# Gathering 32 columns per token block first, and the whole gather behind the first expert pair's gate and up products

## The chip, the core and the metric

The kernel runs on one core of a Trainium2 chip. The core has a matrix engine (PE, with its weight loads shown apart as PEld), a vector engine (DVE), a scalar engine (ACT), GpSimd (POOL), an engine that here only issues transfers (SP), and sixteen DMA engines that bring data from HBM. The engines run their own instruction lists and wait for each other by semaphores. The metric is device time in microseconds for one call; lower is better.

## The reference

The program is two transformer blocks on 256 tokens of 1024 channels, in float32. The first block has two kinds of attention and then a mixture of 32 experts; the second a recurrent mixer and a dense feed-forward network. The change touches the start of the expert layer:

```python
g_sel = argmax(t @ w_group + b_group)                # one of 4 groups for each token
top_v, top_i = top_k(logits of the 8 experts of that group, 2)
w_top = softmax(top_v) * p_group
hg = einsum('nd,edf->nef', t, w_gate)                # each expert: 1024 -> 256
hu = einsum('nd,edf->nef', t, w_up)
a  = silu(hg) * hu * comb[:, :, None]                # comb is 0 but for a token's two experts
y  = einsum('nef,efd->nd', a, w_down)                # 256 -> 1024
```

So only two of 32 experts count for a token, 512 (token, expert) pairs in all.

## The kernel before

The kernel computes only the pairs that are chosen. Each token block (BLK = 2 blocks of 128 tokens) has 256 chosen pairs; a pair gets a column, sorted by expert within its block. `cols` holds each token's two columns. `pick[:, b, :]`, 128 tokens by 256 columns of zeros and ones, is made on DVE by comparing a row of column numbers with `cols` (L2398 to L2405). The gather is a product on PE: for each of KT = 8 tiles of 128 channels and each block, `tok` (normed tokens, 128 tokens by 128 channels) times `pick` gives the block's columns of that tile in a PSUM bank. One bank (512 columns) holds both blocks of one tile, so the gather fills all eight banks with 32 matmuls (L1194 to L1207). ACT moves the even tiles to `xsT` and adds a shift (L1871), DVE the odd ones (L2460).

The experts are then worked off in 16 teams of two (TEAMS). A team's input is a window of 64 columns (WIN): 32 columns (SUB) of each block from the place where its two experts start. `copy_window` (L2446) copies it from `xsT` to `xw`. For the first team it is done in two parts, tiles 0 to 5 and 6 to 7 (FIRST_TILES = 6), so that its products can begin early. If a team has more than 32 columns in a block, a flag selects another, slower branch; here it is the quick one.

One team on the quick branch is: gate and up products in bank 0 (L1210, 32 matmuls with 64-wide stationary tiles and 512 columns), Silu on ACT (L1884), the product of gate and up with the row mask on DVE (L2848), two transposes on PE (`turn_act`, L1270), a copy on ACT (L1889), the down products in bank 2 (L1284, 16 matmuls), and copies of their result by ACT and DVE. While PE is at it, DVE copies the next team's window and makes the matrix that later adds the rows back to their tokens (`put_rows_joined`, L2428). The adding back (L1299) fills gaps of PE.

DVE has a list of its own between the gather and the first Silu: row numbers, masks and weights of all experts (L2475 to L2519). At its end it lets ACT start the first Silu.

The weights of six experts (HOMES) are in SBUF at a time: four in a ring, one in `hs`, one (expert 5, then 11 and so on) partly in `tok`, which is also the gather's input. SP issues the transfers in a written order, each with the wait that frees its place. Around the change: expert 2 (L624), two quarters of expert 5 into `tok`, each behind a part of the gather (L626 to L629), then for experts 6 and 7 the first halves of gate and up, as soon as the first half of the first team's products is done (L638), the second halves when all of them are done (L643), the down weights after the first team's down products (L650), then expert 8 and so on, each after a team's products. Two semaphores carry this: `gate_up_used` and `chunk_used`.

Of the kernel before, what the change touches and what calls it, by code (L numbers as in the profile page):

```python
# [112 lines left out]
FIRST_TILES = 6  # L113
# [42 lines left out]
def build(nc, x, c, w_ada, b_ada, g_mix, w_in, b_forget, g_out_a, g_out_b, w_out, g_ffn, w_group,  # L156
# [3 lines left out]
    with ExitStack() as ctx:  # L160
# [341 lines left out]
        def _(sp):  # L502
# [123 lines left out]
            sp.wait_ge(gather_done, 1)  # L626
            load_quarter(5, 0, 0)
            sp.wait_ge(gather_done, 1 + KT)
            load_quarter(5, 1, 0)  # L629
# [140 lines left out]
        def _(pe):  # L770
# [423 lines left out]
            def gather():  # L1194

                pe.wait_ge(htr_taken_a, 4)
                for b in range(BLK):
                    pe.wait_ge(pick_ready, b + 1)
                    for j in range(KT):
                        if b == 0 and j == 6:  # L1200
                            pe.wait_ge(row_taken, 8)
                        last = pe.matmul(ps[:, j, b * L:(b + 1) * L], lhsT=tok[:, b, j * P:(j + 1) * P], rhs=pick[:, b, :],
                                         start=b == 0, stop=b == BLK - 1, skip_group_check=True)
                        if b == BLK - 1:
                            last.then_inc(gather_done, 1)
                    if b == 0:
                        last.then_inc(gather_done, 1)  # L1207
# [430 lines left out]
            with pe.Else():  # L1638
                gather()
# [25 lines left out]
        def _(act):  # L1665
# [205 lines left out]
            def take_gathered():  # L1871

                for j in range(0, KT, 2):
                    act.wait_ge(gather_done, j + 2)
                    act.activation(xsT[:, j, 0:PAIRS], ps[:, j, :], ACT.Identity, bias=shift_q[:, j:j + 1]
                                   ).then_inc(gather_taken_a, 1)

            def team_act(n, u, fast):
# [1027 lines left out]
```

## Time and profile before

| | us |
|---|---|
| time, median of 3 runs | 766.99 (766.43 to 768.08) |
| profiled execution, its time | 765.26 |
| profiled execution, its span | 762.7 |
| PE busy | 730.6 (96%) |
| DVE busy | 354.0 (46%) |
| ACT busy | 188.0 (25%) |
| POOL busy | 58.8 (8%) |
| mean granted clock of PE | 0.999 of 2.4 GHz |

The span reaches from the first to the last instruction; the time has 2.56 us more around it. The expert layer's stage reaches from some 188 us (routing) to 420 us of the span. A row of a timeline gives start and length in us, engine, line, what is written and read, how often, and in brackets how long the engine was idle before it and what ended the wait.

### The profile page before, as it was taken

What the parts mean: (1) busy time and instruction counts of PE and PEld (TensorE: products, weight loads), DVE (VectorE), ACT (ScalarE), POOL (GpSimd) and SP (SyncE); (2) the same over time, 40 slices, a digit from 0 to 9 for tenths busy, and PEclk for the clock granted to TensorE, in tenths of its full rate; (3) what the DMA queues carried; (4) which work ended last, traced back from release to release, by engine and by line L of the source; (5) the groups of instructions that cost most, each with busy time, mean ns of one, the idle gap of its engine ahead of it and who ended that gap; (6) DMA issues with size and microseconds to landing.
All of it is one profiled execution on the core that took longest, in us unless ns stands there. A gap on an engine that the chain in (4) does not pass through costs nothing.

```text
span 762.7 us, 9761 instructions
## 1 busy us (share of the span) xinstructions
PE 730.6 (96%) x3883; PEld 485.9 (64%) x3883; DVE 354.0 (46%) x798; ACT 188.0 (25%) x412; POOL 58.8 (8%) x69
## 2 busy tenths in 40 slices
PE   6999999998889999999989999999999999999996
PEld 4677778786524434343334886788888888885442
DVE  2125666785721212121121876364276656567445
ACT  5014323533511111111011338131321111111002
POOL 3033660040000000000001000000000000000000
PEclk9999999999999999999999999999999999999999
DMA  9998956956999999999999963123454645443401
GB/s 339 339 339 249 396 192 222 354 205 261 351 377 415 416 414 416 418 413 415 419 409 368 371 227 111 46 66 111 151 181 135 197 146 185 157 175 111 165 28 58
DMA packets 78250, 197.27 MB, mean 259 GB/s; under 512 B 3343, under 2 KB 38520, under 8 KB 72312
## 3 DMA queue, kind: packets, MB, share of 16 engines
q1 hardware_dynamic: 77248, 195.37, 68.6%
q10 hardware_dynamic: 664, 0.80, 0.4%
q0 software_dynamic: 288, 0.41, 0.3%
q8 instruction: 33, 0.54, 0.3%
q14 instruction: 17, 0.14, 0.1%
HBM read 195.33 MB, written 1.05 MB: 257 GB/s over the span
## 4 chain that ended last, share of the span: by engine, by line
PE 75%; SPq 10%; DMA 7%; DVE 5%; ACT 1%; issue 1%; POOL 1%; DVEq 0%; ACTq 0%
PE ps L1502 18%; PE ps L1218 9%; PE ps L777 9%; PE ps L1563 9%; PE ps L1294 5%; PE ps L903 4%; PE ps L1127 4%; SPq L572 4%; PE ps L914 2%; DMA arena<-in_w_up 2%; DMA ring<-in_w_ada 2%; SPq L578 2%; PE ps L1089 2%; PE ps L1099 2%; DMA ring<-in_w_in 2%; PE ps L1303 2%
## 5 line engine op out<-in xcount | busy, mean ns | idle before, releaser
L1218 PE MATMUL ps<-ring,arena 128*64 128x512 f32 x352 | 77.6, 593 | 3.1 <-DMA ring<-in_w_up 2.5
L903 PE MATMUL ps<-hs,ring 128*128 128x256 f32 (+1 forms) x288 | 66.2, 384 | 1.0 <-DMA ring<-in_w_in 1.0
L903 PEld LDWEIGHTS ps<-hs,ring 128*128 128x128 f32 (+1 forms) x288 | 52.7, 187 | 12.7 <-issue 3.8
L1218 PEld LDWEIGHTS ps<-ring,arena 128*64 128x64 f32 x352 | 26.3, 137 | 52.5 <-issue 52.5
L2848 DVE SCALAR_TENSOR_TENSOR arena<-arena,own_rows,ps 128x256 f32<-128x256 f32 x16 | 7.7, 480 | 106.8 <-ACT arena L1884 106.8
L777 PE MATMUL ps<-hs,ring 128*128 128x256 f32 x240 | 53.3, 381 | 0.3 <-PE ps L777 0.3
L777 PEld LDWEIGHTS ps<-hs,ring 128*128 128x128 f32 x240 | 45.2, 190 | 7.1 <-issue 0.9
L1502 PE MATMUL ps<-ring,hs 128*128 128x256 f32 x176 | 41.7, 380 | 0.9 <-DVE xT L2727 0.9
L1502 PE MATMUL ps<-ring,mixT 128*128 128x256 f32 x176 | 41.7, 380 | 0.0
L1502 PE MATMUL ps<-arena,mixT 128*128 128x256 f32 x176 | 41.6, 379 | 0.0
L1294 PE MATMUL ps<-ring,arena 128*64 128x512 f32 x176 | 40.2, 598 | 1.0 <-issue 0.5
L1218 PE MATMUL ps<-hs,arena 128*64 128x512 f32 x80 | 35.2, 592 | 2.2 <-DMA arena<-in_w_up 2.2
L1502 PEld LDWEIGHTS ps<-ring,hs 128*128 128x128 f32 x176 | 33.3, 190 | 6.1 <-issue 1.7
L1502 PEld LDWEIGHTS ps<-arena,mixT 128*128 128x128 f32 x176 | 33.4, 190 | 4.5
L1502 PEld LDWEIGHTS ps<-ring,mixT 128*128 128x128 f32 x176 | 32.6, 190 | 4.0
L1884 ACT ACTIVATE arena<-ps 128x256 f32<-128x256 f32 x16 | 6.1, 384 | 108.4 <-PE ps L1218 100.7
L1127 PE MATMUL ps<-mixT,ring 128*128 128x256 f32 x128 | 28.0, 380 | 0.1
L2690 DVE TENSOR_TENSOR arena<-ring 128x1024 f32<-128x1024 f32 x16 | 19.5, 1220 | 15.7 <-PE ps L1563 15.7
L1294 PEld LDWEIGHTS ps<-ring,arena 128*64 128x64 f32 x176 | 11.9, 136 | 23.1 <-issue 22.4
L1127 PEld LDWEIGHTS ps<-mixT,ring 128*128 128x128 f32 x128 | 24.2, 190 | 3.7 <-issue 0.5
L1218 PEld LDWEIGHTS ps<-hs,arena 128*64 128x64 f32 x80 | 10.9, 137 | 24.4 <-issue 24.4
L2856 DVE COPY arena<-ps 64x512 f32<-64x512 f32 x12 | 8.2, 683 | 36.6 <-PE ps L1294 36.6
(483 smaller groups left out, 1215.5 us busy)
## 6 DMA issues: line engine op xcount, KB each, us to landing
ring<-in_w_down SPq DMA_DIRECT2D x23, 1024.0 KB, 18.1
ring<-in_w_gate_up SPq DMA_DIRECT2D x22, 1024.0 KB, 7.2
ring<-in_w_gate SPq DMA_DIRECT2D x18, 1024.0 KB, 17.1
ring<-in_w_up SPq DMA_DIRECT2D x18, 1024.0 KB, 17.9
ring<-in_w_ada SPq DMA_DIRECT2D x5, 3072.0 KB, 12.9
ring<-in_w_down SPq DMA_DIRECT2D x5, 2048.0 KB, 8.1
ring<-in_w_in SPq DMA_DIRECT2D x9, 1024.0 KB, 17.1
ring<-in_w_ada SPq DMA_DIRECT2D x16, 512.0 KB, 9.3
```

The lines of the kernel that those rows point to most:

```text
L572: sp.dma_start(dst, src[:, e, :]).then_inc(arrived[e % HOMES], 16)
L578: sp.dma_start(dst, src[:, e, D:2 * D] if far else src[:, e, 0:D]).then_inc(arrived[SLOTS + 1], 16)
L777: last = pe.matmul(o, lhsT=w_of(k), rhs=rhs_of(k), start=k == 0, stop=k == k_n - 1)
L903: last = pe.matmul(o[0:n, 0:L], lhsT=w[:, k, lo:lo + n], rhs=h[:, k, :], start=k == 0, stop=k == KT - 1)
L914: last = pe.matmul(o[:, i * n:(i + 1) * n], lhsT=hT[:, k, b * P:(b + 1) * P], rhs=w[:, k, lo:lo + n], start=k == 0, stop=k == KT - 1 and f ...
L1089: last = pe.matmul(ps[:, m // 2, (m % 2) * L:(m % 2 + 1) * L], lhsT=w[:, k, (m % 4) * P:(m % 4 + 1) * P], rhs=mixT[:, k, :], start=m % 2 = ...
L1127: last = pe.matmul(o, lhsT=w[:, k, (m % 4) * P:(m % 4 + 1) * P], rhs=mixT[:, k, :], start=last_of is None and m % 2 == 0 and k % 4 == 0, s ...
L1218: last = pe.matmul(ps[WIN * h:WIN * (h + 1), 0, :].rearrange("p (g n) -> p g n", g=2), lhsT=xw[:, u, k, :], rhs=expert_gate_up(2 * n + h, ...
L1294: last = pe.matmul(ps[WIN * half:WIN * (half + 1), 2, :], lhsT=act_turned[:, u, at:at + WIN], rhs=expert_down(2 * n + h)[:, k, lo:lo + 512 ...
L1502: last = pe.matmul(o, lhsT=tokens(k), rhs=columns(k), start=start and k == 0, stop=k == 3, skip_group_check=True)
L1563: last = pe.matmul(ps[:, DOWN_BANK[name], :], lhsT=lhsT, rhs=rhs, start=n == 0, stop=n == FT // 2 - 1, skip_group_check=True)
L2690: ve.tensor_tensor(sums[0], lo_2, lo_1, ALU.subtract).then_inc(weight_sums, 1)
```

## The change

The first team's window always starts at column 0 of each block, so its columns are known without the window's start. The change makes these 32 columns of each block's pick first and gathers them alone, into halves of two banks (`gather_first`); DVE adds the shift and writes them as the first team's window. The rest of the picks follows on DVE. The first team's gate and up products come next on PE. The whole gather is done in the order of the tiles: two tiles behind those products, six behind the turn of the activations, in banks that are free beside banks 0, 1 and 2 (GATHER_BANKS). Its evictions go between the first team's steps on ACT and DVE, and DVE's second window is copied after them. The down products of the first team now also wait for the tile in bank 2 to be taken. On SP the two quarters of expert 5 that lie in `tok` go behind the second halves of experts 6 and 7 and wait for the whole gather. The slower branch keeps the whole gather; it does the first gather besides.

```diff
-FIRST_TILES = 6
+FIRST_TILES = 4
+GATHER_BANKS = (2, 3, 4, 5, 6, 7, 3, 4)
@@ -623,10 +624,6 @@
-            sp.wait_ge(gather_done, 1)
-            load_quarter(5, 0, 0)
-            sp.wait_ge(gather_done, 1 + KT)
-            load_quarter(5, 1, 0)
@@ -641,6 +638,9 @@
                 if team == HOMES // 2:
                     load_early_halves(1)
+                    sp.wait_ge(gather_done, 2 + KT)
+                    load_quarter(5, 0, 0)
+                    load_quarter(5, 1, 0)
@@ -1191,20 +1191,36 @@
+            def gather_first():
+                pe.wait_ge(htr_taken_a, 4)
+                for half, bank in enumerate((3, 1)):
+                    for b in range(BLK):
+                        if half == 0:
+                            pe.wait_ge(pick_ready, b + 1)
+                        for i in range(FIRST_TILES):
+                            j = half * FIRST_TILES + i
+                            last = pe.matmul(ps[:, bank, i * WIN + b * SUB:i * WIN + (b + 1) * SUB],
+                                             lhsT=tok[:, b, j * P:(j + 1) * P], rhs=pick[:, b, 0:SUB],
+                                             start=b == 0 and i == 0, stop=b == BLK - 1 and i == FIRST_TILES - 1,
+                                             skip_group_check=True)
+                    last.then_inc(gather_done, 1)
+            def gather(tiles):
+                for j in tiles:
+                    if j == 0:
+                        pe.wait_ge(pick_ready, 2 * BLK)
+                        pe.wait_ge(first_windows, 2)
+                    if GATHER_BANKS[j] == 6:
+                        pe.wait_ge(row_taken, 8)
+                    if j >= 6:
+                        before = GATHER_BANKS.index(GATHER_BANKS[j])
+                        pe.wait_ge(gather_taken_v if before % 2 else gather_taken_a, before // 2 + 1)
+                    for b in range(BLK):
+                        last = pe.matmul(ps[:, GATHER_BANKS[j], b * L:(b + 1) * L], lhsT=tok[:, b, j * P:(j + 1) * P],
+                                         rhs=pick[:, b, :], start=b == 0, stop=b == BLK - 1, skip_group_check=True)
+                    last.then_inc(gather_done, 1)
@@ -1614,13 +1630,16 @@
+            gather_first()
             with pe.If(too_many < 1):
-                gather()
                 weights_there(0)
                 gate_up(0, 0, first=True).then_inc(gu_done, 1)
+                gather((0, 1))
                 pe.wait_ge(act_ready, 2)
                 turn_act(0)
+                gather(range(2, KT))
                 pe.wait_ge(turn_taken, 1)
+                pe.wait_ge(gather_taken_a, 1)
                 down_joined(0)
@@ -1868,25 +1887,29 @@
                 act.activation(act_g, ps[:, 0, 0:FE], ACT.Silu).then_inc(silu_done, 1)
+                if first:
+                    take_gathered((0,))
                 act.wait_ge(turn_done, n + 1)
...
                 act.activation(act_turned[:, u, :], ps[:, 1, 0:FE], ACT.Copy).then_inc(turn_taken, 1)
+                if first:
+                    take_gathered((2, 4, 6))
@@ -2396,13 +2418,25 @@
+                ve.tensor_scalar(tmp_cols[:, b * SUB:(b + 1) * SUB], col_no[:, b * L:b * L + SUB], cols[:, 1, b:b + 1], None,
+                                 ALU.is_equal).then_inc(dve_step, 1)
+            for b in range(BLK):
+                own()
+                ve.scalar_tensor_tensor(pick[:, b, 0:SUB], col_no[:, b * L:b * L + SUB], cols[:, 0, b:b + 1],
+                                        tmp_cols[:, b * SUB:(b + 1) * SUB], ALU.is_equal, ALU.add).then_inc(pick_ready, 1)
...
+            for half, bank in enumerate((3, 1)):
+                tiles = slice(half * FIRST_TILES, (half + 1) * FIRST_TILES)
+                ve.wait_ge(gather_done, half + 1)
+                ve.tensor_tensor(xw[:, 0, tiles, :], ps[:, bank, 0:FIRST_TILES * WIN].rearrange("p (k n) -> p k n", n=WIN),
+                                 shift_q[:, tiles].unsqueeze(2).broadcast_to([P, FIRST_TILES, WIN]), ALU.add
+                                 ).then_inc(first_windows, 1)
@@ -2460,18 +2494,14 @@
             starts = load(0, 2 * BLK)
-            take_gathered((1, 3, 5))
-            copy_window(0, starts[0:BLK], slice(0, FIRST_TILES)).then_inc(first_windows, 1)
-            take_gathered((7,))
-            copy_window(0, starts[0:BLK], slice(FIRST_TILES, KT)).then_inc(first_windows, 1)
@@ -2847,7 +2877,11 @@
+                    if n == 0:
+                        put_rows_joined(1)
+                        take_gathered(range(1, KT, 2))
+                        copy_window(1, starts[BLK:2 * BLK]).then_inc(windows_copied, 1)
```

## Rows read from the trace of the kernel before

**Rows 1.** The page's busy times: us, share of the span, instructions.
```profile
PE 730.6 (96%) x3883; PEld 485.9 (64%) x3883; DVE 354.0 (46%) x798; ACT 188.0 (25%) x412; POOL 58.8 (8%) x69
```
**Rows 2.** The chain that ended last, 184 to 420 us: start us, us, what.
```profile
211.80 0.39 ACT arena L1884
...
213.67 3.65 PE ps L1294 x16
217.32 6.89 PE ps L1218 x32
...
371.72 18.31 DMA arena<-in_w_up
```
**Rows 3.** The waits, 185 to 420 us: who, for whom, us, times, longest.
```profile
PE ps L1218 <- DMA ring<-in_w_up: 2.5, 2, 1.8
PE ps L1218 <- DMA arena<-in_w_up: 2.2, 1, 2.2
```
**Rows 4.** Stretches: us, busy times of PE to POOL, PEclk, DMA share, GB/s.
```profile
185.00:190.00 5.00, 2.99 (x27) 2.07 (x24) 3.13 (x11) 1.29 (x4) 0.74 (x1) 1.00 0.86 308
198.00:207.00 9.00, 8.36 (x39) 5.84 (x39) 5.20 (x17) 4.11 (x6) 0.00 (x0) 1.00 1.01 397
207.00:209.00 2.00, 2.00 (x12) 0.86 (x10) 1.73 (x9) 0.00 (x0) 0.00 (x0) 1.00 0.47 193
209.00:213.00 4.00, 2.77 (x14) 0.89 (x10) 2.62 (x11) 0.38 (x1) 0.00 (x0) 1.00 0.88 241
213.00:219.00 6.00, 5.53 (x28) 1.91 (x28) 1.58 (x6) 0.98 (x2) 0.00 (x0) 1.00 1.01 372
...
300.00:390.00 90.00, 85.28 (x396) 34.30 (x392) 17.11 (x56) 11.73 (x29) 0.00 (x0) 1.00 1.02 416
390.00:404.00 14.00, 13.84 (x64) 6.13 (x66) 2.22 (x8) 1.31 (x3) 0.52 (x1) 1.00 1.03 409
```
**Rows 5.** The timeline around the gather and the first team, 191 to 216 us.
```profile
195.31 0.29 DVE L2395 TENSOR_REDUCE arena<-arena 128x4 f32<-128x128 f32 x1
...
196.65 7.14 PE L1202 MATMUL ps<-arena,tok 128*128 128x256 f32 x32 [0.91 <-DVE arena L2404]
...
197.34 0.76 DVE L2409 TENSOR_SCALAR wins_i<-arena 1x32 int32<-1x32 f32 x8
...
204.44 7.09 PE L1218 MATMUL ps<-ring,arena 128*64 128x512 f32 x32 [0.64 <-DVE arena L2449]
...
205.35 0.29 DVE L2477 TENSOR_TENSOR rank<-arena 128x32 f32<-128x32 f32 x2
...
208.12 0.33 SPq L635 DMA_DIRECT2D ring<-in_w_gate  x1
...
212.76 0.44 PE L1273 MATMUL ps<-ident,arena 128*128 128x128 f32 x2 [1.23 <-DVE arena L2848]
```
**Rows 6.** The timeline: rows elsewhere that are nearest to the new operations.
```profile
188.85 1.92 PE L1171 MATMUL ps<-ident,hs 128*128 128x128 f32 x16
...
204.21 0.75 DVE L2464 TENSOR_SCALAR arena<-ps,small 128x512 f32<-128x512 f32 x1
...
208.49 0.86 DVE L2505 SCALAR_TENSOR_TENSOR w_all<-arena,w_all 128x32 f32<-128x32 f32 x4
...
226.72 0.50 DVE L2449 COPY arena<-arena 128x256 f32 x2 [1.49 <-issue]
...
435.76 1.08 DVE L2556 TENSOR_TENSOR arena<-ps,rstd 128x256 f32<-128x256 f32 x3
```
**Rows 7.** Timeline at 224 us; DMA issues (count, KB, landing) of 217, 224, 378.
```profile
224.27 0.34 SPq L572 DMA_DIRECT2D ring<-in_w_gate  x1
...
ring<-in_w_down SPq DMA_DIRECT2D x2, 1024.0 KB, 9.5
...
ring<-in_w_gate SPq DMA_DIRECT2D x1, 1024.0 KB, 6.6
...
ring<-in_w_gate SPq DMA_DIRECT2D x4, 512.0 KB, 15.6
```

More of the change, by code:

```diff
@@ L1192, in _ @@
             quarters(6, ones[:, 0:Q], w[:, PE_K, :], last=True).then_inc(ada_rows_done, 1)
-            def gather():
+            def gather_first():
                 pe.wait_ge(htr_taken_a, 4)
[L1197 to L1207, printed above, removed]
+                for half, bank in enumerate((3, 1)):
[9 more added lines that the diff above has]
+                    last.then_inc(gather_done, 1)
@@ L1638, in _ @@
             with pe.Else():
-                gather()
+                gather(range(KT))
                 clear_banks()
@@ L1869, in _, with take_gathered, team_act @@
             too_many = act.value_load(flag_i[0:1, 0:1], min_val=0, max_val=1)
[L1871 to L1875, printed above, removed]
+            def take_gathered(tiles):
+                for j in tiles:
+                    act.wait_ge(gather_done, j + 3)
+                    act.activation(xsT[:, j, 0:PAIRS], ps[:, GATHER_BANKS[j], :], ACT.Identity, bias=shift_q[:, j:j + 1]
                                    ).then_inc(gather_taken_a, 1)
-            def team_act(n, u, fast):
+            def team_act(n, u, fast, first=False):
                 act.wait_ge(gu_done, n + 1)
@@ L2048, in _ @@
             with act.If(too_many < 1):
-                take_gathered()
                 for n in range(TEAMS):
-                    team_act(n, n % 2, True)
+                    team_act(n, n % 2, True, n == 0)
                 second_block()
             with act.Else():
-                take_gathered()
+                take_gathered(range(0, KT, 2))
                 with act.Fori(0, TEAMS * WINDOWS) as i:
@@ L2398, in _ @@
             for b in range(BLK):
-                if b:
-                    ve.wait_ge(pick_ready, b)
-                half, found = col_no[:, b * L:(b + 1) * L], tmp_cols
+                ve.tensor_scalar(tmp_cols[:, b * SUB:(b + 1) * SUB], col_no[:, b * L:b * L + SUB], cols[:, 1, b:b + 1], None,
[4 more added lines that the diff above has]
+                                        tmp_cols[:, b * SUB:(b + 1) * SUB], ALU.is_equal, ALU.add).then_inc(pick_ready, 1)
+            for b in range(BLK):
+                ve.wait_ge(pick_ready, BLK + b)
+                half, found = col_no[:, b * L + SUB:(b + 1) * L], tmp_cols[:, SUB:L]
                 ve.tensor_scalar(found, half, cols[:, 1, b:b + 1], None, ALU.is_equal).then_inc(dve_step, 1)
                 own()
-                ve.scalar_tensor_tensor(pick[:, b, :], half, cols[:, 0, b:b + 1], found, ALU.is_equal, ALU.add
+                ve.scalar_tensor_tensor(pick[:, b, SUB:L], half, cols[:, 0, b:b + 1], found, ALU.is_equal, ALU.add
                                         ).then_inc(pick_ready, 1)
+            for half, bank in enumerate((3, 1)):
[4 more added lines that the diff above has]
+                                 ).then_inc(first_windows, 1)
             starts_4d = starts_f.rearrange("p (b q h) -> p b q h", b=BLK, h=2)
@@ L2462, in take_gathered @@
                 for j in tiles:
-                    ve.wait_ge(gather_done, j + 2)
-                    ve.tensor_scalar(xsT[:, j, 0:PAIRS], ps[:, j, :], shift_q[:, j:j + 1], None, ALU.add
+                    ve.wait_ge(gather_done, j + 3)
+                    ve.tensor_scalar(xsT[:, j, 0:PAIRS], ps[:, GATHER_BANKS[j], :], shift_q[:, j:j + 1], None, ALU.add
                                      ).then_inc(gather_taken_v, 1)
@@ L2859, in _ @@
             with ve.Else():
+                take_gathered(range(1, KT, 2))
                 ve.memset(put[:, 0], 0.0).then_inc(dve_step, 1)
```

2 lines of the change are left out of this document (1 added, 1 removed).

## Prediction

> **What bounds the kernel now.** I read the page's busy shares first: PE is busy for 96% of the span and every other engine for less than half of it [rows 1]. That looks like a kernel whose every microsecond of PE counts, so I next read the chain that ended last over the expert stage, 184 to 420 us [rows 2]. It runs over PE with steps of ACT between them at first (the Silu at 211.80, the down products at 213.67, the next team's gate and up products at 217.32), but further on it leaves PE: it goes through SP's issues and a transfer, "DMA arena<-in_w_up", of 18.31 us from 371.72. The waits say the same in small: between 185 and 420 us gate and up products waited for weights three times, 2.5 us on ring tiles (two waits) and 2.2 us on an arena tile [rows 3]. So by 390 us PE has caught up with the weight stream, and the end follows the stream and not PE. The table of stretches shows why: from 300 to 390 us the sixteen DMA engines move 416 GB/s with a share of 1.02 [rows 4]. A team's weights are six transfers of 1024 KB, 6.29 MB, or 15.1 us at 416; a team's products take some 12.9 us on PE (two starts of gate and up, 204.44 [rows 5] and 217.32 [rows 2], are 12.88 apart). PE lives on a head start that is used up at 390.
>
> The question is therefore what the change does to the stream, and the place to look is the only stretch behind the gather that is not full: 207 to 209 with 193 GB/s and a share of 0.47, 209 to 213 with 241 and 0.88, 213 to 219 with 372 and 1.01 [rows 4]. SP sits before the first early halves until the first half of the first team's gate and up products is done; they go out at 208.12 [rows 5], when the queue has run dry.
>
> **The change part by part. PE and DVE first, as they set SP's issues.**
> The columns of the tokens are known when the reduction of 195.31 ends, 195.60 [rows 5]. Before, two full pick rows follow until 197.34 (1.74 us), and the gather starts in their midst at 196.65.
>
> *Short picks (added):* four operations of 32 columns; the nearest row has four of 128x32 in 0.86 [rows 6]. First pick after three of them, 196.25, second 196.46. PE starts some 0.15 after the first: 196.4.
>
> *First gather (added):* 16 matmuls with 128-wide stationary tiles and 32 moving columns. No row has them. Bounds: the 16 transposes with the same stationary width in 1.92, and the full gather, 32 in 7.14, that is 0.223 each [rows 5, 6], so 1.9 to 3.6 us. I take 1.9, since 32 columns are nearer to the transposes' 128 than to 256. First half done at 197.4, second at 198.3.
>
> *Rest of the picks (moved behind):* 224 of 256 columns, so at most the 1.74 of before, from 196.46 to 198.2. DVE, not PE, is late here. Then two adds from PSUM of 128x256, three of which took 1.08 [rows 6]: 198.6 and 198.95. They stand where the gather's evictions and the two window copies stood.
>
> *Gate and up products of the first team* start at 198.7 instead of 204.44 [rows 5], 5.7 earlier, and end 7.1 later at 205.8. PE's branch now stands between first gather and products; the 0.4 us in which PE waits for DVE cover it.
>
> *DVE's list to the first Silu (not changed, but now exposed):* the window starts, eight short operations in 0.76 [rows 5], the register loads, bounded by the 1.49 us idle "issue" ahead of a window copy in the team loop [rows 6], and then everything from 205.35 [rows 5] to the Silu at 211.80 [rows 2], 6.45. From 198.95: 198.95 + 0.76 + 1.49 + 6.45 = 207.65, say 207.7. The products end at 205.8, so PE's two gather tiles (4 matmuls, 0.9) fit into the wait for nothing, and of the 5.7 us only 211.80 - 207.7 = 4.1 are left. This is the new wait that takes the gather's place.
>
> *Rest of the gather (moved):* the first two tiles cost nothing, by that wait. The other 12 matmuls, 12 x 0.223 = 2.7, stand between turning the activations and the down products. Before, the turn started 0.96 after the Silu (212.76 [rows 5]) and down 1.87 after it (213.67). Now 207.7 + 0.96 + 0.2 + 2.7 = 211.55: a gain of 2.1 against 213.67. ACT's copy of the turned activations is beside it.
>
> *Evictions (moved):* on DVE after its product (Silu + 0.9) and the put rows (0.9): four of 0.75 [rows 6], the last not before the gather's end, so 212.5, then the second window, 213.1; wanted by PE at 211.55 + 3.65 = 215.2. ACT's four lie beside. Cost nothing, with a cover of 2 us; beyond it they would hold the second team.
>
> *SP:* both quarters of expert 5 (team 2) leave the place ahead of the early halves and go behind them, past the wait for the whole gather (211.6). Behind that wait stand only the loads of team 3's down weights, which wait for the first down products (215.2) anyway. The first early halves go out 3.7 after the products' start as before (208.12 - 204.44 [rows 5]): 202.4; the second at 205.9. Team 2's products come at 227, the quarters land before 220.
>
> **The sum.** PE's gain at the second team is 2.1 us, and with it the issue of expert 8's weights, 224.27 before [rows 7], moves to 222.1. For the stream: bytes moved from 198 to 209 are 9 x 397 + 2 x 193 = 3960 KB [rows 4]; without the 1050 of the quarters the queue runs dry at 205.1, but the early halves are there from 202.4 and the second from 205.9. The dry stretch disappears. It is worth 2 x (1 - 193/416) + 4 x (1 - 241/416) = 1.07 + 1.68 = 2.75 us; 213 to 219 holds another 6 x (1 - 372/416) = 0.63 with full shares, which I leave where it is. Does the stream then run dry later, at expert 8? Before, its first transfer, issued at 224.27, landed 6.6 later at 230.9, and the last down weights before it at about 228.3 (issued to 218.9, 9.5 in the mean) [rows 7]; one transfer of 1024 KB takes 2.5, so its bytes began when those of the earlier ones ended, about 226.4 to 227 if a landing trails its bytes by 1 to 2 us. An issue moves bytes about 1 us later (208.12, after which 207 to 209 stayed at 193): it was early by 1 to 2 us. With 2.1 of PE's gain on top, the stream may gain up to 3.1 before it waits for SP. So the stream gains 2.75, and PE's waits at its end [rows 3] shrink or grow to fit. After 390 the second half of the kernel follows shifted, as its first weights stand in the same queue.
>
> The profiled execution took 765.26: 762.7 of span and 2.6 around it. Forecast for it: 762.5. It lies 1.7 below the median of the runs, 766.99; on that footing the forecast is 766.99 - 2.75 = 764.2.
>
> Rule against the change: the moved transfers are 512 KB, and 241 GB/s is what the stretch of such pieces shows [rows 4]. The Trainium skill ("DMA: Bandwidth & Descriptors", section Bandwidth) advises batching to 1 MiB or more for at least 75% of peak. By that the slow 209 to 213 would be the price of the small pieces and stay, and only the 1.07 of 207 to 209 would be won. The trace speaks against it: the last teams' eight halves of 512 KB, issued from 378 on behind others and landed 15.6 us later in the median [rows 7], move in a full stream, 409 GB/s from 390 to 404 [rows 4]. It is the empty queue, I think, not the size.
>
> **Rivals.**
> *A. The stream keeps its shape:* the slow stretch belongs to the pieces themselves and comes back a few us earlier. For it: shares of 0.88 and 1.01 at 241 and 372 GB/s are busy engines. Against: 409 in 390 to 404. Gain at most 1.07: 765.9, or nothing at all.
> *B. The whole lead reaches the end:* the 5.7 us at the first products carry through: 761.3. Against it are DVE's list to 207.7 and three waits for weights [rows 3].
> *C. The products start earlier, DVE's list does not shrink:* first gather at 3.6 us and slow register loads put the Silu at 209.1 or later; PE gains 0.7, and the stream, bound by expert 8's issue, 1.7 to 2.7: 765.3 at most. It is the low end of the forecast's own range.
> *D. Slower: TensorE's clock.* PE now waits for the picks' adds (0.4 us) and some 2 us ahead of the turn. If after this the clock falls to the lower level (1.2 GHz), the 12 matmuls and the down products take twice their 2.7 + 3.65, PE loses 6.35 - 2.1 = 4.2, and from the 1 to 2 us by which expert 8's issue was early it is the stream that loses, 2.7 at the middle: 769.7. Against: from 185 to 190 PE was busy for 2.99 of 5 us and the granted clock stayed at 1.00, the full 2.4 GHz; so in all rows shown [rows 4]. The Trainium skill ("TensorE: Matmul & The Clock Gate", section Why this matters for your kernels) warns of idle gaps between bursts; no gap of this case's stretch made it happen.
>
> **How the numbers follow.** Forecast with C 0.65 (gain 1.7 to 3.4), A 0.23, B 0.05, D 0.07. A measurement of this kernel can tell about 0.2%, 1.5 us. Faster by more: nearly all of the first and B, 0.67. Within: A and a rest, 0.25. Slower: D and a part of the unknown, 0.08. Range: below, a gain of 3.4 (all of 207 to 219) and 0.8 for the spread of the runs, 762.8; above, A with no more than 0.5 won, 766.5.
>
> **What would show it.** In the changed profile: first products at about 198.7 and the Silu about 207.7, released by DVE and not by PE; twelve gather matmuls just before the first down products at about 211.5; second team's products at 215.2; no second between 204 and 215 with less than 300 GB/s; the last wait for weights at about 387 instead of 390. The prediction is wrong if the slow second stretch is still there, if expert 8's weights go out later than 224, or if the granted clock leaves 1.00.

## The result: slower, by 0.4%

The changed kernel takes 768.99 us (median of 10 runs, 767.41 to 771.53), the one before 766.17 beside it (10 runs, 764.74 to 768.08): ratio 1.0042, 95% interval 1.0028 to 1.0056. The forecast was 764.2. The profiled execution took 767.41, with a span of 764.6; before 765.26 and 762.7. It is the fastest of its ten, so the tables below show 1.9 of the 2.8 us between the medians. The page's busy line, to be held against [rows 1]:

```profile
PE 736.3 (96%) x3915; PEld 489.7 (64%) x3915; DVE 353.5 (46%) x800; ACT 187.9 (25%) x412; POOL 59.0 (8%) x69
```

PE has 32 records more than before, 3915 against 3883, and 5.7 us more of busy time.

The view to compare next is PE's timeline around the gather (start, length, engine, line, operation, tiles, count; in brackets the idle time ahead and what ended it). L1203 is the first gather, L1234 gate and up, L1221 the rest of the gather, L1289 the turn, L1310 the down products:

```profile
196.22 3.73 PE L1203 MATMUL ps<-arena,tok 128*128 128x32 f32 x32 [0.58 <-DVE arena L2425]
199.88 8.78 PE L1234 MATMUL ps<-ring,arena 128*64 128x512 f32 x32
208.60 1.99 PE L1221 MATMUL ps<-arena,tok 128*128 128x256 f32 x8
210.43 0.38 PE L1289 MATMUL ps<-ident,arena 128*128 128x128 f32 x2
210.65 5.35 PE L1221 MATMUL ps<-arena,tok 128*128 128x256 f32 x24
215.92 3.65 PE L1310 MATMUL ps<-ring,arena 128*64 128x512 f32 x16
219.41 7.04 PE L1234 MATMUL ps<-ring,arena 128*64 128x512 f32 x32
```

The first products did move forward, from 204.44 to 199.88 [rows 5]. But the first down products moved back, from 213.67 [rows 2] to 215.92, and the second team, 217.15 in the same view of the kernel before, to 219.41 ([rows 2] has 217.32 from the chain, which counts a piece from the end of the one ahead of it):

```profile
217.15 7.04 PE L1218 MATMUL ps<-ring,arena 128*64 128x512 f32 x32
```

The rows also show why: the source has 16 products in the first gather and 12 in the rest of it, and the trace has 32 and 24 records. In every group of products here one product is two matmul records: gate and up are 16 in the source and 32 here, the down products 8 and 16. Only the transposes of the turn have one record each, 2 and 2. The "32 matmuls" and "16 matmuls" in the section on the kernel before are therefore records, and the full gather's 32 are 16 products.

DVE, ACT and SP's queue in the same stretch:

```profile
198.20 0.42 DVE L2437 TENSOR_TENSOR arena<-ps,small 128x256 f32<-128x256 f32 x1 [0.24 <-PE ps L1203]
199.99 0.42 DVE L2437 TENSOR_TENSOR arena<-ps,small 128x256 f32<-128x256 f32 x1 [1.36 <-PE ps L1203]
202.92 0.29 DVE L2507 TENSOR_TENSOR rank<-arena 128x32 f32<-128x32 f32 x2 [1.83 <-issue]
209.37 0.38 ACT L1903 ACTIVATE arena<-ps 128x256 f32<-128x256 f32 x1 [10.10 <-DVEq L2548]
205.27 0.33 SPq L632 DMA_DIRECT2D ring<-in_w_gate  x1
208.75 0.33 SPq L632 DMA_DIRECT2D ring<-in_w_gate  x1
216.02 0.33 SPq L579 DMA_DIRECT2D tok<-in_w_gate  x1
219.62 0.89 SPq L600 DMA_DIRECT2D ring<-in_w_down  x2
226.53 0.34 SPq L573 DMA_DIRECT2D ring<-in_w_gate  x1
```

DVE waits 1.36 us for the second half of the first gather; from 202.92 its list takes the forecast 6.45 us, and the Silu is let go by DVE's list ("DVEq"), at 209.37. On SP the early halves leave at 205.27 and 208.75, the quarters at 216.02, team 3's down weights at 219.62, and expert 8's weights at 226.53, 2.26 later than before [rows 7]. What that does to the weight stream stands in the table of stretches (length; busy time of each engine; PE's granted clock; DMA share; GB/s):

```profile
198.00:207.00 9.00, 9.00 (x44) 4.16 (x45) 5.16 (x28) 1.26 (x2) 0.00 (x0) 0.81 0.81 330
207.00:209.00 2.00, 2.00 (x10) 0.67 (x7) 1.46 (x6) 0.00 (x0) 0.00 (x0) 1.00 0.92 252
209.00:213.00 4.00, 4.00 (x21) 3.48 (x20) 2.35 (x7) 2.14 (x4) 0.00 (x0) 1.00 0.96 341
213.00:219.00 6.00, 6.00 (x30) 3.36 (x30) 2.33 (x5) 1.37 (x2) 0.00 (x0) 1.00 1.02 376
219.00:229.00 10.00, 8.98 (x46) 3.18 (x44) 1.56 (x4) 1.91 (x5) 0.00 (x0) 1.00 0.92 342
300.00:390.00 90.00, 87.44 (x406) 35.04 (x402) 16.43 (x55) 11.14 (x28) 0.00 (x0) 1.00 1.02 416
```

Against a full 416 GB/s these stretches are short by 9 x (1 - 330/416) = 1.86, 0.79, 0.72, 0.58 and 1.78 us, 5.7 together. Before, 198 to 219 were short by 0.41, 1.07, 1.68 and 0.63 [rows 4], 3.8, and 219 to 229 ran at 416. The difference is 1.9 us, as large as that of the spans. It comes out at the last wait for weights, of team 14:

```profile
PE ps L1234 <- DMA ring<-in_w_up: 2.3, 2, 1.8
PE ps L1234 <- DMA arena<-in_w_up: 2.1, 1, 2.1
```

The waits look as before (2.5 and 2.2 [rows 3]), which is the point: PE still waits, only later. Team 14's products start at 392.20; before at 390.16 (the first row is the kernel before, the second the changed one):

```profile
390.16 0.61 PE L1218 MATMUL ps<-hs,arena 128*64 128x512 f32 x1 [2.16 <-DMA arena<-in_w_up]
392.20 0.61 PE L1234 MATMUL ps<-hs,arena 128*64 128x512 f32 x1 [2.12 <-DMA arena<-in_w_up]
```

Up to there PE is not the bound; it only decides when SP may issue.

### The profile page after: what moved, and what is told of

Read it like the earlier page. It is cut to its first block, busy times and chain, and to the rows that moved or that the text cites. A ratio compares the mean times of both kernels' runs of the same rounds, so it can differ in the third digit from the quotient of the medians.

```text
span 764.6 us, 9824 instructions
## 1 busy us (share of the span) xinstructions
PE 736.3 (96%) x3915; PEld 489.7 (64%) x3915; DVE 353.5 (46%) x800; ACT 187.9 (25%) x412; POOL 59.0 (8%) x69
## 4 chain that ended last, share of the span: by engine, by line
PE 76%; SPq 10%; DMA 7%; DVE 4%; ACT 1%; POOL 1%; issue 1%; ACTq 0%; DVEq 0%
PE ps L1518 17%; PE ps L1234 10%; PE ps L777 9%; PE ps L1579 9%; PE ps L1310 5%; PE ps L903 4%; PE ps L1127 4%; SPq L573 4%; PE ps L914 2%; DMA arena<-in_w_up 2%; DMA ring<-in_w_ada 2%; SPq L579 2%; PE ps L1089 2%; PE ps L1099 2%; DMA ring<-in_w_in 2%; PE ps L1319 2%
## 5 line engine op out<-in xcount | busy, mean ns | idle before, releaser
L1234 PE MATMUL ps<-ring,arena 128*64 128x512 f32 x352 | 79.2, 603 | 2.3 <-DMA ring<-in_w_up 2.3
L903 PEld LDWEIGHTS ps<-hs,ring 128*128 128x128 f32 (+1 forms) x288 | 52.7, 187 | 12.9 <-issue 3.8
L1234 PEld LDWEIGHTS ps<-ring,arena 128*64 128x64 f32 x352 | 26.3, 139 | 53.1 <-issue 53.0
L1310 PE MATMUL ps<-ring,arena 128*64 128x512 f32 x176 | 40.2, 598 | 0.5 <-issue 0.5
L1234 PE MATMUL ps<-hs,arena 128*64 128x512 f32 x80 | 35.2, 592 | 2.1 <-DMA arena<-in_w_up 2.1
L1234 PEld LDWEIGHTS ps<-hs,arena 128*64 128x64 f32 x80 | 10.9, 137 | 24.4 <-issue 24.4
L1310 PEld LDWEIGHTS ps<-ring,arena 128*64 128x64 f32 x176 | 11.9, 136 | 22.7 <-issue 22.7
```

The lines of the kernel that those rows point to most:

```text
L903: last = pe.matmul(o[0:n, 0:L], lhsT=w[:, k, lo:lo + n], rhs=h[:, k, :], start=k == 0, stop=k == KT - 1)
L1234: last = pe.matmul(ps[WIN * h:WIN * (h + 1), 0, :].rearrange("p (g n) -> p g n", g=2), lhsT=xw[:, u, k, :], rhs=expert_gate_up(2 * n + h, ...
L1310: last = pe.matmul(ps[WIN * half:WIN * (half + 1), 2, :], lhsT=act_turned[:, u, at:at + WIN], rhs=expert_down(2 * n + h)[:, k, lo:lo + 512 ...
```

## The experiments

The experiments were timed in four groups, each beside the kernel before, whose medians were 767.54, 767.16, 767.22 and 767.02 us; a ratio is always to the kernel before of the same group. Two things had to be explained: which of PE's steps made SP late, and what the granted clock did, which fell to 0.51 between 200 and 202 with PE busy for all of it:

```profile
198.00:200.00 2.00, 2.00 (x20) 1.96 (x21) 0.43 (x2) 1.26 (x2) 0.00 (x0) 1.00 1.05 434
200.00:202.00 2.00, 2.00 (x6) 0.57 (x8) 1.09 (x9) 0.00 (x0) 0.00 (x0) 0.51 0.96 401
202.00:204.00 2.00, 2.00 (x8) 0.63 (x6) 0.98 (x6) 0.00 (x0) 0.00 (x0) 0.63 1.00 412
```

That is why the first team's products took 8.78 us and not 7.09.

**1. The first gather with 128 columns (FC) instead of 32.**

```diff
-                                             lhsT=tok[:, b, j * P:(j + 1) * P], rhs=pick[:, b, 0:SUB],
+                                             lhsT=tok[:, b, j * P:(j + 1) * P], rhs=pick[:, b, 0:FC],
```

> The changed kernel with a first gather that moves 128 columns of each block's pick instead of 32 (the same 32 weight loads, so the same 3.7 us on PE; only the first 32 columns of each 128 are used). Theory K (clock): the granted clock falls after the first gather because its matmuls move few columns, although PE is shown busy without a gap. Then here the clock stays at 1.00 between 198 and 207 us, the first gate and up products take 7.1 us instead of 8.8, all runs have a mean clock of 0.998 or more, none of 0.994, and the median falls by 0.5 to 1.5 us, from 769 to about 768, with less spread. Rival (the waits of PE around the first gather let the clock fall, whatever the columns): the clock falls as before, 8.8 us, and the median stays at 769. In both, the down products of the first team start at 215.5 to 216, since the number of matmuls on PE's path is the same.

Measured: 770.19 us, ratio 1.0026 (1.0012 to 1.0039). The clock stays up in this stretch:

```profile
196.59 3.81 PE L1204 MATMUL ps<-arena,tok 128*128 128x128 f32 x32 [0.78 <-DVE arena L2426]
200.32 7.09 PE L1235 MATMUL ps<-ring,arena 128*64 128x512 f32 x32
```

Four times the columns cost 0.08 us more: a record takes 0.119 instead of 0.117. Between 32 and 128 columns it is therefore not the moving columns that set its price. The 128x128 stationary tile, which both have in common, is the likely reason; no run has a narrower one with as few columns. The Trainium skill ("TensorE: Matmul & The Clock Gate", section LDWEIGHTS (loading the stationary operand)) puts a stationary load at P / 1.2 ns, where P is its number of columns; for 128 columns that is an estimate of 107 ns. The 117 and 119 ns here lie some 10% above it. With the clock kept, the first halves go out at 204.02 instead of 205.27, but the Silu is not earlier (209.88, still by DVE's list), nor are the down products (216.38) and expert 8 (226.99). So in the result's profile the fall of the clock was all but hidden behind DVE's list: the turn comes 1.06 us after the Silu there and 0.95 here, so PE lost 0.1 us by it. The rest of theory K did not come: the mean clocks of the twelve runs are 0.994 to 0.998, and the median is not near 768. The ratio is a little below the result's 1.0042, but the intervals overlap.

**2. Half of the moved gather.** Tiles 2 to 7 take the first token block alone, 12 records instead of 24; the second block's columns of these tiles are left out.

```diff
-                    for b in range(BLK):
+                    for b in range(BLK if j < 2 else 1):
```

> The changed kernel, whose gather of tiles 2 to 7 leaves out the second token block (6 of 12 products, 12 of 24 matmuls in the trace; the expert layer's output is then not the reference's). Theory P (path): the part of the gather behind the turn stands on PE's path in full, at twice the length that I had forecast, since each product is two matmuls. Then it takes 2.7 us instead of 5.35, the first down products start at about 213.2 instead of 215.9, expert 8's weights go out at about 223.9 instead of 226.5, and the median falls by 1.5 to 2.7, to 766.3 to 767.5. Theory S (the transfers' order on SP makes the loss): the median stays at 768.5 to 769.5, as SP's order is untouched.

Measured: 767.92 us, ratio 0.9996 (0.998 to 1.0012), some 0.46% below the changed kernel.

```profile
210.81 2.76 PE L1221 MATMUL ps<-arena,tok 128*128 128x256 f32 x12
213.50 3.65 PE L1310 MATMUL ps<-ring,arena 128*64 128x512 f32 x16
```

The records that went, 2.6 us, came off the start of the down products (213.50) and of expert 8's issue (224.11; before it was 224.27). The rest of the gather is on the path, at 0.223 a record.

**3. The quarters' move alone**, on the kernel before.

```diff
-            sp.wait_ge(gather_done, 1)
-            load_quarter(5, 0, 0)
-            sp.wait_ge(gather_done, 1 + KT)
-            load_quarter(5, 1, 0)
...
                     load_early_halves(1)
+                    sp.wait_ge(gather_done, 1 + KT)
+                    load_quarter(5, 0, 0)
+                    load_quarter(5, 1, 0)
```

> The kernel before with SP's part of the change alone: the two quarters of expert 5 go behind the second early halves. PE, DVE and ACT are untouched, so expert 8's weights go out at 224.3 as before. Theory S: the queue runs dry from 205 instead of 208 until the early halves start at 209, and the stream never gets the 2.5 us back: 767.2 to 768.8. Theory P: the stream was 1 to 2 us early at expert 8, so it loses at most 1 us: 766.2 to 767.2.

Measured: 768.08 us, ratio 1.0012 (1.0 to 1.0024), a small loss at most.

```profile
206.00:210.00 4.00, 4.00 (x20) 1.56 (x18) 3.53 (x16) 0.00 (x0) 0.00 (x0) 1.00 0.17 50
219.00:229.00 10.00, 8.97 (x46) 3.32 (x42) 1.83 (x7) 1.32 (x4) 0.00 (x0) 1.00 1.03 416
```

Without the quarters the queue is nearly empty from 206 to 210. Expert 8 leaves at 224.25, as before, and yet team 14 starts at 392.79 in this profile, 168.5 us after that issue instead of the 165.9 of before (390.16 - 224.27). Bytes lost early are lost as well, when the queue never runs dry again behind them. That is theory S in the profile; the ratio by itself does not tell the two theories apart.

**4. The changed kernel again**, one execution.

> The changed kernel once more, for a second profile. Theory K: the fall of the clock after the first gather is there again, and if it lasts longer (a mean clock of 0.994 instead of 0.997) the first products take more than 10 us, the Silu is then released by PE and not by DVE, and the time is 2 to 3 us longer than that of the first profile, 767.4. If the mean clock is the same, so are time and products.

770.0 us; first gather 3.73, clock down at 200.8, expert 8 at 227.01, team 14 at 393.66: the same picture with the same 8.78 us for the first products, and yet a span of 767.3, 2.7 us more. Of these 0.5 lie ahead of the expert layer (the transposes of rows 6 start at 189.24; in the result at 188.76), 1.0 in the weight stream and 1.2 behind team 14's start. Single profiles differ by that much.

**5. The kernel before again**, one execution.

> The kernel before once more, as a second profile of it, to see how much one profile differs from the next in the places that I compare: the issue of expert 8's weights (224.27 in the first), the bytes moved in 207 to 213, and the start of team 14's products after their last wait for weights (390.16). I expect the first two within 0.5 us and the third within 1.5 us.

765.84 us; expert 8 at 224.67, team 14 at 390.99, 166.3 later. The low stretches lie elsewhere: 198 to 207 has 365 GB/s and 207 to 209 has 340, where the first profile had 397 and 193 [rows 4]. Short of a full stream, 198 to 219 is much the same, 4.0 us and 3.8.

**6. The changed kernel, with team 4's weights in halves,** the first of them as soon as half of the second team's products is done.

```diff
+                if team == HOMES // 2 + 1:
+                    sp.wait_ge(part_used, 4 + 1)
+                    load_part(2 * team, 0, D)
```

> The changed kernel, in which the weights of experts 8 and 9 (team 4) are loaded in halves: the first halves as soon as half of team 1's gate and up products is done, not all of them. PE, DVE and ACT are as in the changed kernel. Theory D (the stream is as late as the last time its queue ran dry before it stays full; in the changed kernel that is ahead of expert 8's weights, since PE frees their place 2.2 us later): the first halves go out at about 223 instead of 226.5 to 227, the dry stretch of 218 to 229 is gone, and the time falls by 1.5 to 3 us to about that of the kernel before, a ratio of 0.999 to 1.001. Rival P2 (the end follows PE's first down products, which stay 2.2 us late): the ratio stays at 1.003 to 1.004.

768.34 us, ratio 1.0023 (1.0009 to 1.0037), between what the two theories gave. Expert 8's first half leaves at 223.72 instead of 226.5 to 227.0, and 219 to 229 still moves only 349 GB/s, probably as it waits behind down weights that left at 220.28.

**7. The kernel before with the same and with team 3's first halves in two parts.**

```diff
+            sp.wait_ge(part_used, 4 + 1)
+            load_part(HOMES, 0, D // 2)
             sp.wait_ge(gate_up_used, 1)
-            load_early_halves(0)
+            load_part(HOMES, D // 2, D)
```

> The kernel before with transfers let go in smaller steps: the first halves of experts 6 and 7 in two parts (after two and after four of the eight tiles of the first team's products), and experts 8 and 9 in halves as in a_release8. PE, DVE and ACT are those of the kernel before. Theory D: the part that goes out at about 206.3 fills the dry stretch of 207 to 209, and the halves at about 221 keep the queue full at expert 8; the stream is 1.5 to 2.7 us earlier, and so is the end: a ratio of 0.9965 to 0.998. Rival P2: no difference, 0.999 to 1.001, as PE's first team is untouched.

766.09 us, ratio 0.9992 (0.998 to 1.0003). Expert 8's first half leaves at 220.69, team 14 starts at 389.76, 0.4 before that of the first profile of the kernel before and 1.2 before that of experiment 5. The ratio lies in what the rival P2 gave and not in theory D's range. In the profiled execution the gain is eaten by the clock, which falls when PE starts again behind its wait for team 14's weights:

```profile
388.00:390.00 2.00, 0.24 (x2) 0.23 (x4) 0.33 (x1) 0.23 (x1) 0.00 (x0) 1.00 1.04 414
390.00:392.00 2.00, 2.00 (x8) 0.78 (x6) 0.00 (x0) 0.00 (x0) 0.00 (x0) 0.65 1.02 408
392.00:394.00 2.00, 2.00 (x6) 0.61 (x4) 0.00 (x0) 0.00 (x0) 0.00 (x0) 0.50 1.03 410
```

**8. Experiment 1 with four tiles of the gather ahead of the turn** instead of two, so that PE has no wait there.

```diff
-                gather((0, 1))
+                gather(range(4))
```

> The changed kernel with the wide first gather of e1_wide (128 columns) and four tiles of the whole gather ahead of the turn instead of two, in the time in which PE waits for DVE's list. Both theories expect the first down products at about 214.6 instead of 216.4 and expert 8's weights at about 225.2 instead of 227.0; by D and by P2 alike the time falls by 1 to 2 us against e1_wide (ratio to the kernel before about 1.0005 against 1.0026). If the rest of the gather did not count, the ratio would stay at 1.002 or more.

770.03 us, ratio 1.003 (1.0012 to 1.0047): nothing won at the median. But the profile and the median show executions in which the clock fell more often: the four runs with a mean clock of 0.998 or more took 766.27 to 768.04, against 767.78 to 768.9 for the four of experiment 1 with 0.998. Among these, something was won, as expected. In the profile the Silu came at 210.93, so down stood at 215.73 in spite of it, and expert 8 at 226.33; PE's clock had fallen already at 189.3 in this execution, ahead of everything that was changed.

**9. The down products first.** In the changed kernel only tile 2 stays ahead of the first down products, tiles 3 to 7 go behind them, and the quarters behind team 3's down weights.

```diff
                 turn_act(0)
-                gather(range(2, KT))
+                gather((2,))
                 pe.wait_ge(turn_taken, 1)
                 pe.wait_ge(gather_taken_a, 1)
                 down_joined(0)
+                gather(range(3, KT))
```

> The changed kernel with one order turned round on TensorE: after the turn of the first team's activations only gather tile 2 is done, then the first down products, then tiles 3 to 7; the quarters of expert 5 go out behind team 3's down weights. Theory P (the lost time is the 24 records that stand before the first down products): these products start at about 211.7 instead of 215.9, team 3's down weights go out at 215.3 instead of 219.6, and the time falls back to that of the kernel before, ratio 0.998 to 1.001. Theory R (the stream follows the last issue that finds the queue dry, and that is expert 8's): the gather's rest still has to be done before the second team, whose products now wait for the last eviction and window as well and start at about 221 instead of 219.4; expert 8 goes out at about 228, team 14 starts about 1.2 us later than in the changed kernel, ratio 1.005 to 1.007.

771.6 us (six runs), ratio 1.0053 (1.0033 to 1.0073). Theory P is refuted:

```profile
196.52 4.99 PE L1204 MATMUL ps<-arena,tok 128*128 128x32 f32 x32 [0.58 <-DVE arena L2427]
201.44 9.11 PE L1235 MATMUL ps<-ring,arena 128*64 128x512 f32 x32
213.49 3.65 PE L1311 MATMUL ps<-ring,arena 128*64 128x512 f32 x16
223.13 7.09 PE L1235 MATMUL ps<-ring,arena 128*64 128x512 f32 x32 [1.48 <-DVE arena L2485]
```

The down products are at 213.49, earlier than in the changed kernel, and the kernel is no faster. The gather has to be done ahead of the second team wherever it stands; that team now starts at 223.13, expert 8 leaves at 230.30, and team 14 starts at 395.77, 165.5 later. Expert 8's issue is 2 us later than theory R expected. In this execution the clock was down for longer, already within the first gather (4.99 us), so here it did cost time.

**10. The same with releases in parts,** as in 6 and 7 (team 4 in three).

> As f0, and the weights that overwrite a team's slots go out in parts as its products go on: team 3's first halves in two parts (after two and after four of the eight contraction steps of the first team), team 4's in three (after two, four and eight steps of the second team). Theory R: expert 8's first part goes out at about 223 and finds the queue still filled, the dry stretches between 198 and 229 shrink below those of the kernel before (3.8 us against a full stream), team 14 starts at 388.5 to 389.5, ratio 0.996 to 0.9985. Theory P: no faster than f0. Either way a fall of TensorE's clock behind the wait for team 14's weights can give 1.7 us back.

769.7 us, ratio 1.0024 (1.0012 to 1.0037): 1.9 us better than 9, so earlier issues helped here, but no better than 6. Theory R's number was missed. The first products were late by the clock as in 9 (the second team at 223.31), and 213 to 219 and 219 to 229 still moved only 354 and 364 GB/s.

**11. The changed kernel, timed beside 9 and 10.**

> The changed kernel itself beside the others on the same chip: 1.003 to 1.0055, expert 8 at 226.5 to 227, and its executions in two sets some 2.5 us apart by the mean granted clock.

770.67 us, ratio 1.0048 (1.0029 to 1.0067): the result again. Executions in which the clock hardly fell show that the loss does not need it: with a mean clock of 0.999 the changed kernel took 768.76 and 769.45, the kernel before beside it 765.32 to 765.94.

**12. Experiment 7, timed again.**

> The kernel before with team 3's first halves in two parts and team 4's in two, measured again with more rounds: theory R gives 0.998 to 0.9995, as the queue's dry stretches hold about 0.6 us less; without it, 1.000.

766.77 us, ratio 0.9995 (0.9981 to 1.0008). With 7 it makes two measurements a little below 1, neither clear of it.

**13. The changed kernel with the prediction's counts:** first gather and tiles 2 to 7 with the first token block alone, 16 and 12 records; the second block's part of both is left out.

```diff
-                        for i in range(FIRST_TILES):
+                        for i in range(FIRST_TILES if b == 0 else 0):
...
-                    for b in range(BLK):
+                    for b in range(BLK if j < 2 else 1):
```

> The changed kernel with as few gather records as the prediction counted: the first gather takes the first token block alone (16 records instead of 32), tiles 2 to 7 too (12 instead of 24); what is left out is the second token block's part of both, so the output is another. It asks whether the forecast of 764.2 (ratio 0.996 to 0.997) would have come true with a right count. Theory R (the stream ends 166 us after expert 8's issue, or later if the queue ran dry before): Silu at about 207.9, first down products at 211.8, expert 8 at 222.4, hence team 14 at 388.4 to 389.5 and a ratio of 0.9965 to 0.999. Theory Q (moving the quarters behind the early halves costs by itself what it cost alone, 1.8 us against the kernel before in the profiles): team 14 at 390 to 392, ratio 0.9995 to 1.002.

765.09 us, ratio 0.9979 (0.9968 to 0.999): faster, by 1.9 us at the medians, where the forecast had 2.75.

```profile
196.84 1.94 PE L1203 MATMUL ps<-arena,tok 128*128 128x32 f32 x16 [0.58 <-DVE arena L2425]
199.05 7.09 PE L1234 MATMUL ps<-ring,arena 128*64 128x512 f32 x32 [0.27 <-DVE arena L2437]
209.43 2.75 PE L1221 MATMUL ps<-arena,tok 128*128 128x256 f32 x12
212.12 3.65 PE L1310 MATMUL ps<-ring,arena 128*64 128x512 f32 x16
209.00:213.00 4.00, 3.84 (x18) 2.71 (x20) 3.71 (x9) 2.61 (x5) 0.00 (x0) 1.00 1.02 412
213.00:219.00 6.00, 6.00 (x30) 2.01 (x28) 1.18 (x3) 0.59 (x1) 0.00 (x0) 1.00 1.02 412
219.00:229.00 10.00, 8.97 (x44) 3.41 (x42) 2.54 (x8) 1.91 (x5) 0.00 (x0) 1.00 1.03 410
```

This is nearly the profile that was predicted: first gather 1.94 (forecast 1.9), products at 199.05 (198.7), down at 212.12 (211.55), expert 8 at 222.72 (222.1), and no stretch of low GB/s from 209 on. The four transfers of 512 KB that left from 206.2 run at 412 here. The span is 762.1, 0.6 shorter than in the first profile of the kernel before, though the expert layer starts 0.5 later in it (the transposes of rows 6 at 189.38; before 188.85).

**14. Experiment 7 finer still:** team 3's halves in four parts, its down weights each when its place is free.

```diff
+            sp.wait_ge(part_used, 4 + 2)
+            load_part(HOMES, D, D + D // 2)
...
+                if team == HOMES // 2:
+                    sp.wait_ge(part_used, 4 + 3)
+                    load_down(2 * team)
```

> The kernel before with all releases finer and the gather untouched: team 3's halves in four parts (after two, four, six and eight steps of the first team's products), its two down weights each as the first team's down products of that expert are done, team 4's halves in two. Theory R: the queue's dry stretches between 207 and 219 shrink by some 1.1 us against the version with parts alone; team 14 starts at 388.5 to 389.5, ratio 0.9965 to 0.9985, and a fall of TensorE's clock behind the wait there takes up to 1.7 us of it back. If SP's issues (0.45 us each, 20 in a row) hold the stream instead: 0.999 to 1.0005.

766.96 us, ratio 1.0 (0.9988 to 1.0013), in the range of the second expectation.

```profile
209.00:213.00 4.00, 2.78 (x15) 0.87 (x11) 2.59 (x12) 0.39 (x1) 0.00 (x0) 1.00 0.96 283
213.00:219.00 6.00, 5.53 (x28) 1.86 (x29) 1.67 (x6) 0.98 (x2) 0.00 (x0) 1.00 1.03 354
```

The issues went out earlier and the GB/s did not rise, at a share of 1.03. These pieces are of 256 KB; whether SP's row of issues or the size of the pieces holds them was not separated and stays open. No version that does all of the work was found clearly faster than the kernel before.

**What the runs say together.** The spans end 372.4 to 372.7 us after team 14's start in eight profiles (before, 5, the result, 6, 10, 11, 13, 14), and 374.1 to 374.4 after it in five where the clock fell behind that wait (2, 3, 7, 9, 12), some 1.7 later. Of the other three, 4 has 373.6 (it waits 0.73 us for down weights at 417) and 1 and 8 have 375.5 and 375.6, a fall of the clock and 1.3 us that I could not place. Team 14's start in turn stands a nearly fixed time, 165.5 to 166.7 us, behind expert 8's issue in most of the profiles in which the queue was not full at that issue:

| | expert 8 leaves | team 14 starts | difference |
|---|---|---|---|
| before / 5 | 224.27 / 224.67 | 390.16 / 390.99 | 165.9 / 166.3 |
| result / 4 / 11 | 226.53 / 227.01 / 226.88 | 392.20 / 393.66 / 393.05 | 165.7 / 166.7 / 166.2 |
| 1 | 226.99 | 393.30 | 166.3 |
| 9 | 230.30 | 395.77 | 165.5 |
| 13 | 222.72 | 389.71 | 167.0 |
| 8 | 226.33 | 393.93 | 167.6 |
| 2 / 3 | 224.11 / 224.25 | 391.86 / 392.79 | 167.8 / 168.5 |

In the last three lines team 14 comes later than that issue asks for. In 13 and 3 the queue was full by then (410 and 416 GB/s from 219 to 229), and bytes lost earlier decide; in 2 and 8 it was not (370 and 340), so the account is not exact. The reading that fits most profiles has two limits, expert 8's issue and the bytes lost before it, and has the kernel before near both at once: its queue is full from 219 to 229 [rows 4], and its difference is as small as where the queue was not full. It is argued from the profiles and not shown.

The experiments that let expert 8 go in parts speak against the issue of its first part as a limit. In 6, 7, 12 and 14 the first halves left some 3.4 us earlier, and team 14 came 169.0, 169.1, 169.0 and 170.2 after them; behind the second halves (227.20, 224.17, 226.13 and 224.37) it came 165.5, 165.6, 165.5 and 166.8. The second halves leave when PE ends the second team's gate and up products. Whether their issue holds team 14, or something else that moves with PE's second team, was not separated; only 10, where team 14 came 163.6 behind the last parts, speaks for the issue.

## Why the prediction was wrong

**First gather: the step that failed first.** "16 matmuls ... I take 1.9" counted the products of the source and paid for them with a price per record: the full gather's 32 records in 7.14 us are 16 products [rows 5]. The right count is 32 records, 3.73 us. By records the bounds would have been 3.8 to 7.1 us, and the lower one, from the transposes' 1.92 for 16 records [rows 6], is the right price. The Silu comes at 209.37, 1.7 after the forecast: 1.4 of it by the first gather and the adds behind it, 0.3 by DVE's register loads (1.83 instead of 1.49).

**Rest of the gather: the second, larger part of the same error.** "The other 12 matmuls, 12 x 0.223 = 2.7" are 24 records, 5.35 us. (The two tiles ahead of the turn, "4 matmuls, 0.9", are 8 and 1.99; they still fit into the wait, but for 0.1.) The sum with both mended, 211.55 + 1.7 + 2.65 = 215.9, is the measured 215.92. Instead of 2.1 us earlier PE is 2.25 later at the down products. Experiment 2 takes away the second part of the error, and the loss is gone; experiment 13 takes away both, and there the sign of the forecast holds.

**DVE's list and the evictions** were right: DVE releases the Silu, and the evictions and the second window do not hold the second team (no wait ahead of 219.41).

**SP:** the moved quarters harmed no one who waits for them, team 2, but their bytes were missing while the early halves were not yet allowed. "The early halves are there from 202.4" failed with the clock and the first gather (205.27). And the margin, "it was early by 1 to 2 us", was none: of the 2.26 us by which expert 8 is late in the result 2.04 come out at team 14, and of 6.03 in experiment 9 5.61. The landing times, from which it had been worked out, didn't show it.

**The sum.** That the stream sets the end was right up to team 14's start: PE waits for weights there in all profiles. Behind that wait PE sets the end, and a fall of the clock there comes out in full, 1.7 us. With as few records as the prediction counted, the kernel is faster by 1.9 us instead of 2.75 (experiment 13). A team's 12.9 us on PE mixed two views: by the timeline alone (204.44 and 217.15) they are 12.7, and nothing in the sum rests on it.

**The rivals.** A is refuted for 512 KB (412 GB/s in 13). B did not happen. C had the first gather's size right (3.6, Silu at 209.1 or later) but kept the wrong rest. D had the sign, and a fall of the clock did come, but neither where it had it nor as the cause: it lies in the first team's products, not behind a wait, and in experiment 1 and in the runs of experiment 11 with a mean clock of 0.999 the loss is there without it.

## What to carry to other kernels

Take a count from the same place as its price: if a row gives 32 records in 7.14 us, count records of that row and not products of the source. A step that only reorders PE's work in a kernel bound by a weight stream is worth what it does to the issues of transfers; list for each release when its place becomes free, before and after, up to the first one behind which the queue stays full. Look for both late issues and lost bytes: experiments 7, 12 and 14 brought issues forward in a kernel that may stand at both, and won next to nothing.

## What had not been expected of the hardware

The granted clock fell to 1.2 GHz while PE is shown busy without a gap, from 196.22 on. In seven profiles the first gather had 32-column records in their full number: the clock fell at 198.7 to 200.8 in six of them (the result, 4, 6, 9, 10, 11), and not in one (2). With half as many records (13) it did not fall there, nor with 128-column records (1 and 8). In the result's timed runs it was free, too: two with a mean granted clock of 0.999 took 768.03 and 768.12, the profiled one with 0.997 took 767.41. The five with 0.994 took 769.6 to 771.5. What fell a second time in them is not shown, as no profile of the changed kernel has it; in seven profiles of the other experiments (1, 2, 3, 7, 8, 9, 12) it is the fall behind the wait of 2.1 to 3.1 us for team 14's weights, which costs 1.7 us since nothing hides it. The kernel before seems to have it as well: its profiles, with a mean clock of 0.999, show no fall there, but beside experiment 1 its three runs with 0.999 took 765.15 to 765.9, and eighteen with 0.997 took 767.1 in the mean. This spread is as large as the change that was to be measured.
